# Layer 0's recurrent unit: gates by tanh of half the argument, two one-column activations, and another order of slab parts

## What is computed

```python
u, gate, xq = split(h @ w_in)                       # 512 features each
u = causal_conv4(u) + conv_b
r = sigmoid(block_diag(u, w_r) + b_r)
i = sigmoid(block_diag(u, w_i) + b_i)
log_a = -8 * r * softplus(-lam)
a = exp(log_a)
b = sqrt(-expm1(2 * log_a)) * (i * u)
hs = scan(a, b)                                     # h_t = a_t * h_(t-1) + b_t
y = hs * gelu(gate)
x = x + concat([y, memory_attention(xq, mem)]) @ w_out
```

## Time and profile before

| | us |
|---|---|
| median of 3 runs (lowest, highest) | 2771.75 (2771.39, 2772.77) |
| the profiled execution | 2773.09 |
| its span | 2771.5 |
| PE matmuls busy | 2716.5 |
| DVE busy | 1589.3 |
| ACT busy | 987.8 |

### The profile page before, as it was taken

How to read it: one execution, slowest core, us unless ns; L and a number is a source line. 1 busy time by engine, 2 the same in 40 slices (tenths; PEclk the granted TensorE clock), 3 DMA queues, 4 the chain that set the end, 5 groups by cost and what they waited for, 6 DMA issues and landing times.

```text
span 2771.5 us, 45703 instructions
## 1 busy us (share of the span) xinstructions
PE 2716.5 (98%) x19386; PEld 2259.8 (82%) x19386; DVE 1589.3 (57%) x2334; ACT 987.8 (36%) x1364; POOL 187.6 (7%) x272
## 2 busy tenths in 40 slices
PE   9999999999999999999999999999999999999999
PEld 7878888898688888877878888888878878888887
DVE  5668777864667777665563553333585454633334
ACT  5643222244632222354342432223543433422223
POOL 4000000000000000001050000000010220000000
PEclk9999999999999999999999999999999999999999
DMA  4334555522045555320023233232220133233231
GB/s 158 107 114 125 183 173 172 162 75 76 3 135 182 165 173 165 96 92 27 3 83 105 91 98 100 92 106 80 76 71 4 33 92 103 81 101 97 92 102 65
DMA packets 239934, 281.19 MB, mean 101 GB/s; under 512 B 9718, under 2 KB 227330, under 8 KB 239746
## 3 DMA queue, kind: packets, MB, share of 16 engines
q1 hardware_dynamic: 226426, 226.29, 25.5%
q0 software_dynamic: 13184, 52.11, 6.4%
q10 hardware_dynamic: 136, 0.03, 0.0%
HBM read 276.31 MB, written 2.10 MB: 100 GB/s over the span
## 4 chain that ended last, share of the span: by engine, by line
PE 88%; DVE 5%; ACT 3%; issue 2%; POOL 1%; DMA 0%; DVEq 0%; SPq 0%; ACTq 0%; POOLq 0%
PE psum L2583 25%; PE psum L2584 24%; PE psum L2585 24%; DVE wlo L1668 1%; PE psum L2664 1%; PE psum L3195 1%; PE psum L2666 1%; PE psum L2665 1%; PE psum L3180 1%; PE psum L3163 1%; ACT whi L933 1%; PE psum L3219 1%; PE psum L2598 1%; PE psum L3152 1%; POOL mo L881 0%
## 5 line engine op out<-in xcount | busy, mean ns | idle before, releaser
L2583 PE MATMUL psum<-hh,whi 128*128 128x512 f32 (+1 forms) x2016 | 781.0, 387 | 4.7 <-DVE wlo L1668 4.3
L2584 PE MATMUL psum<-hl,whi 128*128 128x512 f32 (+1 forms) x2016 | 772.0, 383 | 0.0
L2585 PE MATMUL psum<-hh,wlo 128*128 128x512 f32 (+1 forms) x2016 | 772.0, 383 | 0.0
L1668 DVE TENSOR_TENSOR wlo<-raw,whi 128x2048 fp32r<-128x2048 f32 x217 | 501.6, 2311 | 457.9 <-ACT whi L933 457.5
L933 ACT ACTIVATE whi<-raw 128x2048 fp32r<-128x2048 f32 x217 | 414.4, 1910 | 521.0 <-PE psum L2585 516.8
L2583 PE MATMUL psum<-mh,whi 128*128 128x512 f32 (+1 forms) x1248 | 485.3, 389 | 1.3 <-issue 1.0
L2584 PE MATMUL psum<-ml,whi 128*128 128x512 f32 (+1 forms) x1248 | 479.1, 384 | 0.0
L2585 PE MATMUL psum<-mh,wlo 128*128 128x512 f32 (+1 forms) x1248 | 479.0, 384 | 0.0
L2583 PEld LDWEIGHTS psum<-hh,whi 128*128 128x128 f32 x2016 | 379.3, 188 | 91.7 <-issue 8.7
L2585 PEld LDWEIGHTS psum<-hh,wlo 128*128 128x128 f32 x2016 | 379.3, 188 | 74.4
L2584 PEld LDWEIGHTS psum<-hl,whi 128*128 128x128 f32 x2016 | 379.6, 188 | 72.5 <-issue 0.5
(11 more groups left out here) (482 smaller groups left out, 2782.3 us busy)
## 6 DMA issues: line engine op xcount, KB each, us to landing
rest<-in_ada_w POOLq DMA_DIRECT2D x64, 768.0 KB, 5.3
raw<-in_w_gu SPq DMA_DIRECT2D x44, 1024.0 KB, 5.1
raw<-in_w_in SPq DMA_DIRECT2D x34, 1024.0 KB, 5.3
raw<-in_w_mlp_in SPq DMA_DIRECT2D x32, 1024.0 KB, 5.4
raw<-in_w_mlp_out SPq DMA_DIRECT2D x32, 1024.0 KB, 5.1
raw<-in_w_out SPq DMA_DIRECT2D x16, 1024.0 KB, 5.0
raw<-in_w_down SPq DMA_DIRECT2D x16, 1024.0 KB, 4.9
raw<-in_w_mem_kv SPq DMA_DIRECT2D x8, 1024.0 KB, 5.1
```

Of the source, the lines that this page charges most:

```text
L1668: ins = dve.tensor_tensor(wlo[:, g % 2, :, :], raw[:, g % 2, :, :], f32(whi[:, g % 2, :, :]), ALU.subtract)
L2583: pe.matmul(out, whi_, xhi, start=first, stop=False)
L2584: pe.matmul(out, whi_, xlo, start=False, stop=False)
L2585: return pe.matmul(out, wlo_, xhi, start=False, stop=last)
```

## The change

- Both gates are computed with Tanh at scale 0.5 and a halved bias (`half_b`). sigmoid(x) is (1 + tanh(x/2)) / 2. The missing "1 +" and factors of one half are put into later operations: `RB` is multiplied by and added to half of `nsp` (one instruction with two operations), `IB` gets 1.0 added before it is multiplied by u, and the root is taken of a quarter of its argument.
- DVE makes `half_b` (two instructions on 128x4) after the vectors have arrived, and `half_nsp` (one on 128x4, with a wait for it) after the softplus.
- ACT gets a Sqrt of one column ahead of its wait for `lru_1ma2`, and an Exp of one column behind the root. Their results are not used.
- ACT runs `hi` of memv 0,1 before the gelu of gate tiles 2 and 3 and no longer behind it.
- DVE runs `lo` of memv 1,0 in round 2 (was 1), of memv 1,1 in round 4, behind that round's scan (was 3), and of wo 0 in round 6 (was 5).
- The padding shrinks by what the three new small tiles take, so that no other tile moves.

```diff
@@ -439,7 +439,10 @@
         gqk = sb("gqk", [P, 2])
         lf = sb("lf", [P, 2, NT * FOX_H], F32R)
         g_first = sb("g_first", [P, KT])
-        sb("padding", [P, 72])
+        spare = sb("spare", [P, 8])
+        half_b = sb("half_b", [P, 2, 4])
+        half_nsp = sb("half_nsp", [P, 4])
+        sb("padding", [P, 52])
 
         e = ExitStack()
         hh = sb("hh", [P, KT, T], F32R, e)
@@ -1141,14 +1144,15 @@
                     hi(slab_of("memv", 0, 0))
                     gate_out(0)
                     mem_high(1)
+                    hi(slab_of("memv", 0, 1))
                     gate_out(1)
-                    hi(slab_of("memv", 0, 1))
-
+
+                    act.wait_ge(S("half_bias"), 2)
                     for t in range(4):
-                        for dst, name, b in ((RB, "rgate", "b_rgate"), (IB, "igate", "b_igate")):
+                        for n, (dst, name) in enumerate(((RB, "rgate"), (IB, "igate"))):
                             j = J[name, t]
                             ready(act, j)
-                            free(act.activation(dst[:, t, :], bank(j), ACT.Sigmoid, bias=V(b, t)), j)
+                            free(act.activation(dst[:, t, :], bank(j), ACT.Tanh, scale=0.5, bias=half_b[:, n, t:t + 1]), j)
                     act.wait_ge(S("lru_loga"), 4)
                     act.activation(U[:, :, 0:T], RB, ACT.Tanh, scale=-1.0).then_inc(S("lru_tanh"), 1)
                     act.wait_ge(S("lru_tanh"), 1)
@@ -1157,8 +1161,10 @@
                     evac_tokens("memv", 0, mV[0], MT_, [0], high=False)
                     evac_tokens("memv", 0, mV[0], MT_, [1], high=False)
                     hi(slab_of("memk", 1, 1))
+                    act.activation(spare[:, 0:1], ident[:, 0:1], ACT.Sqrt)
                     act.wait_ge(S("lru_1ma2"), 4)
-                    act.activation(U[:, :, 0:T], U[:, :, 0:T], ACT.Sqrt).then_inc(S("lru_root"), 1)
+                    act.activation(U[:, :, 0:T], U[:, :, 0:T], ACT.Sqrt, scale=0.25).then_inc(S("lru_root"), 1)
+                    act.activation(spare[:, 1:2], ident[:, 0:1], ACT.Exp)
 
                     def beside_units(i):
 
@@ -1911,6 +1917,9 @@
                     scaled("u", 1, lambda t: U[:, t, 3:T + 3])
                     vec_out(1)
                     vec_out(2)
+                    for n, name in enumerate(("b_rgate", "b_igate")):
+                        c = VEC[name][0]
+                        dve.tensor_scalar(half_b[:, n, :], vec[:, c:c + 4], 0.5, None, ALU.mult).then_inc(S("half_bias"), 1)
                     c = VEC["mu_shift_2"][0]
                     q.mark(dve.tensor_scalar(omm[:, :], vec[:, c:c + 2 * SHIFT_TILES], -1.0, 1.0, ALU.mult, ALU.add))
                     dve.wait_ge(s_const, 4)
@@ -1948,6 +1957,9 @@
                     lo(slab_of("memk", 0, 1))
                     dve.wait_ge(S("lam_exp"), 1)
                     softplus_tail(tiny[:, 4, 0:4], tiny[:, 3, 0:4], tiny[:, 5, 0:4], tiny[:, 6, 0:4], tiny[:, 7, 0:4], nsp[:, :], -8.0)
+                    q.settle()
+                    q.mark(dve.tensor_scalar(half_nsp[:, :], nsp[:, :], 0.5, None, ALU.mult))
+                    q.settle()
                     lo(slab_of("gate", 0, 0))
                     lo(slab_of("gate", 0, 1))
                     scaled("gate", 0, lambda t: G[:, t, :])
@@ -1960,9 +1972,10 @@
                     lo(slab_of("memv", 0, 1))
                     for t in range(4):
                         evacuated(dve, J["rgate", t])
-                        dve.tensor_scalar(RB[:, t, :], RB[:, t, :], nsp[:, t:t + 1], None, ALU.mult).then_inc(S("lru_loga"), 1)
+                        dve.tensor_scalar(RB[:, t, :], RB[:, t, :], half_nsp[:, t:t + 1], half_nsp[:, t:t + 1], ALU.mult, ALU.add)\
+                           .then_inc(S("lru_loga"), 1)
                     evacuated(dve, J["igate", 3])
-                    dve.tensor_tensor(IB, IB, UC, ALU.mult).then_inc(S("lru_iu"), 1)
+                    dve.scalar_tensor_tensor(IB, IB, 1.0, UC, ALU.add, ALU.mult).then_inc(S("lru_iu"), 1)
                     dve.wait_ge(S("lru_a"), 1)
                     dve.tensor_tensor(DB, RB, RB, ALU.mult).then_inc(S("lru_a2"), 1)
                     lo(slab_of("memk", 1, 0))
@@ -1975,7 +1988,7 @@
 
                         if i == 0:
                             lo(slab_of("memk", 1, 1))
-                        if i == 1:
+                        if i == 2:
                             lo(slab_of("memv", 1, 0))
                         if 1 <= i < 5:
                             t = i - 1
@@ -1989,9 +2002,9 @@
                             dve.wait_ge(S("lru_scan"), t + 1)
                             dve.wait_ge(S("gelu"), 4)
                             dve.tensor_tensor(UC[:, t, :], UC[:, t, :], G[:, t, :], ALU.mult).then_inc(S("lru_y"), 1)
-                        if i == 3:
+                        if i == 4:
                             lo(slab_of("memv", 1, 1))
-                        if i == 5:
+                        if i == 6:
                             lo(slab_of("wo", 0, 0))
                         for t in range(4) if i == 8 else ():
                             dve.wait_ge(S("lru_hi"), t + 1)
```

## The result

The changed kernel takes **2819.43 us** (median of 4 runs, 2813.94 to 2819.93), beside 2771.91 us for the kernel before. The ratio is 1.0167, with a 95% interval of 1.0155 to 1.0178. It is 1.7% slower, 54 us above the forecast and far outside the range. Yet the stretch that I reasoned about moved as I said.

A forecast was written before the change was run, and what follows sets the result against it. PE, busy for 98% of the span, was taken as the bound, so only its waits before `wo` could give time. 1.85 + 2.6 + 1.0 + 1.0 = 6.45 us took 2771.75 to 2765.3, range 2763.6 to 2769.0 (8 in 10).

The forecast's parts named there:

- The step that failed: PE begins `wo` at 174.97 us and goes through it without a gap; bringing that start forward brings the rest forward.
- It doesn't do what it says: Rival: a load appears elsewhere in the stretch or PE's clock falls in a new gap; under 2 us, 2771.0; chance 0.03.
- Gates: On ACT, with `hi` moved and the load before them gone, the gates start at 109.0 (or 110.3).
- the three cases for the loads: ACT's table loads up to the exp: row 3.2 us shorter in the first two cases, 1.9 in the third.
- PE's floor: PE ends the gate matmuls at 111.49, so memv 0 starts there for 113.04: 1.55 us and no more.
- The root's wait: ACT's wait of 0.72 us for DVE before the root is gone, and ACT is the later one.
- The one-column activations: ACT's short Sqrt and Exp at the root only add themselves, 0.21 us each, within bounds of 0.1 and 0.4.
- The rounds: In the attention, DVE's waits for ACT's `hi` at three moved `lo` go: 2.6 + 1.0 + 1.0 us gained.
- the front: ACT's row up to the exp, then the root and first exponential: 1.55 + 0.72 - 0.42 = 1.85 us gained.
- The tightest place: On PE, the fifth unit's scores end at about 142.5 against the reduction at 143.35: 0.9 us.
- the rounds give nothing: Rival: DVE's waits pass to PE or ACT's exponentials, leaving only the front's 1.85 us: 2769.9; chance 0.12.
- the front gives nothing: Rival: one-column activations cost far more or an extra load is added, leaving the rounds' 4.6 us: 2767.1; chance 0.12.

The follow-up runs named there:

- tiles back: The changed kernel with its padding cut from 52 to 48 words, so its tiles stand where they did in the kernel before: 2764.23 us, ratio 0.9974.
- all +32: The kernel before with 8 words put ahead of raw, so weights, constants and activations all stand 32 bytes further on: 2772.06 us, ratio 1.0000.
- its weights moved: The changed kernel with raw, weights and constants 32 bytes further on, its activations left where the change put them: 2765.49 us, ratio 0.9976.
- before +32: The kernel before with its padding at 80 words for 72, so the activation tiles stand 32 bytes further on: 2826.65 us, ratio 1.0192.
- before -32: The kernel before with its padding at 64 words, so the activation tiles stand 32 bytes nearer the start: 2825.71 us, ratio 1.0202.
- weights +32: The kernel before with 8 words ahead of raw and padding at 64: weights and constants 32 bytes further on, activations in place: 2823.84 us, ratio 1.0192.

## Why the prediction was wrong, and what of it was right

**The step that failed** is at the start: "All that the change touches lies before that start, and what brings `wo` forward brings the rest forward". It rests on the last point of the section on the change, that no other tile moves, and on taking PE's 98% of busy time as fixed, so that only its waits could change. What the runs showed in its place: the tiles moved by 32 bytes, each product of 512 columns in the whole kernel took 233.3 ns for 226.9, and what follows the start of `wo` grew by 52.78 us. Four words less of padding took the loss away. I had added up sizes and never looked at where the tiles come to stand. Had I seen the 32 bytes, nothing in the trace of before would have priced them: its operands all stand at a distance of 0 modulo 128. But they would have been a part of the change with an open cost on more than 9000 products of 512 columns (three times 1888 + 1184 in the groups above), and a rival. No rival of mine reached past `wo`. "It doesn't do what it says" came nearest, with under 2 us.

The size fits. After lies 55.2 us above itself with its tiles back, and its span is 55.7 us longer. Behind the start of `wo`, the products of 512 columns with these tiles take 55.3 us more, added up from the start of each to the start of the next, and all the rest 0.7 us less; the products of 256 columns, each step of theirs 1.7 ns shorter, give back only 0.1 us with the waits among them. Before the gate matmuls 1.25 us are lost.

**The steps inside the stretch held.** With the tiles back it is 7.0 us shorter, against a sum of 6.45. The differences to before count from the start of the gate matmuls, 104.46 there and 104.00 here; the other times are starts in the profile:

- *Gates.* Their start was given as 4.54 us in (109.0 - 104.46), and is 4.54 (108.54 - 104.00). The first of the three cases for the loads came true.
- *PE's floor.* 1.55 was forecast. ACT's last copy out of memv 0, at 122.58, comes 1.79 earlier, so this term was too small by 0.24. The first product of memv 0 now overlaps the end of the gate matmuls, where it followed an idle time before.
- *The root's wait* of 0.72 us is gone. *The one-column activations* cost 0.11 each, not 0.21: a row lasts 0.20, but the next begins 0.11 after its start. 1.79 + 0.72 - 0.22 = 2.29, and the first exponential is 2.28 earlier. I read a row's duration as its price, though rows overlap. The table loads run ahead of the wait, as I took it: in the run without the one-column activations the root's load starts 0.6 us before DVE is through with the root's input. The Trainium skill, "ScalarE: Activation LUTs", section "Step-by-step: what each stage is for", has the load stand right before the ACTIVATE that needs it; read as behind that instruction's wait, the Sqrt would have been a gain, and no run here shows one.
- *The rounds* were forecast at 2.6 + 1.0 + 1.0 = 4.6 and give 4.65, as the rest beside the front. The first L1808 is 8.3 us earlier, where I had 7.6; the 0.4 from the front are part of it.
- *The tightest place* was the fifth unit's scores. They end at 141.45 (rows at 140.42, 1.03 long) against a reduction at 142.26, so 0.8 us of slack, for 0.9 forecast. PE's three idle times are gone. It waits for DVE or ACT only in the last rounds, the 0.67 and 0.34 us above among them.

Without the moved tiles the forecast of 2765.3 would have been 1.1 us off. The rivals "the rounds give nothing" (2769.9) and "the front gives nothing" (2767.1) fall by the runs that undo the parts. Most of what the sum of 6.45 lacks to the 7.0 us is found: 0.20 for the two short activations, 0.24 at PE's floor, 0.05 in the rounds. That is no excuse for the 54 us: it was the change as written that was to be forecast.

## What to carry to other kernels

A change of tiles in SBUF is a change of the whole program: print the addresses of both builds, with the rounding, before forecasting a local gain, and look at the mean duration of the commonest matmul in a far stretch before any local row. A kernel that computes with two tiles in step should hold their distance on purpose, not by a padding that happens to come out right; here 32 bytes cost seven times what the whole change gained. And parts that look additive need not be: the front's 2.4 us were worth 0.4 to 1.3 until the order of the slab parts closed PE's gap.

## What the runs showed of the hardware

- **Pace and distance of operands.** Products of 128x512 with a weight load for each start every 226.9 ns in the mean when streamed tiles and weight tiles stand a multiple of 128 bytes apart (before, all +32, after with its tiles back or its weights moved), every 233.3 ns when they are 32 or 96 off (after, before +32, before -32, weights +32), and every 229.0 ns at 64, by pair of tiles 227.4 to 230.1. With `wlo` alone moved the three pairs differ, 228.3 to 238.8, and the mean is 233.3. Products of 256 columns with the same tiles go the other way: 119.6 ns at 0, 117.7 to 117.9 at 32 or 96, 115.4 at 64. The mechanism stays open.
- **The clock at a gap.** With the order undone it fell to 0.50 within the gap of 3.48 us, and came back only after PE had worked for 5.7 us. In the profiled run of the kernel before it held through the gap of 2.73 us and behind it (1.00 from 144 to 148). In that of all +32, whose gap at the same place is 2.74 us, it fell after PE had begun again (0.57 in the mean from 144 to 148). Of the eight profiles with the code of before, moved tiles or not, whose gaps there are 2.73 to 2.95 us, five lost the clock and three kept it. So whether the kernel before loses clock there can differ from run to run. The windows of before, then of all +32:

```profile
144.00:148.00 4.00, 4.00 (x30) 3.74 (x29) 3.71 (x8) 2.74 (x7) 0.00 (x0) 1.00 0.00 0
```
```profile
144.00:148.00 4.00, 4.00 (x23) 4.00 (x22) 3.90 (x8) 2.07 (x7) 0.00 (x0) 0.57 0.03 9
```

- **The clock and the spread.** All +32 has a stretch 0.9 us longer than before, so that gap can explain little of why the runs of before spread from 2766.56 to 2776.76 us. The clock over the whole span goes with it: runs with a mean granted clock of 0.998 took 2767 us in the mean, those with 0.994 took 2775.
- **One table for gelu and tanh.** No load stands between the gelu and the gates' tanh in any run with the change's gates.
